# One-hot rows for the second pair of experts, sums in two groups of banks, and identity products in eleven waits of TensorE

## What is computed

```python
for i in range(2):                       # layers 0 and 1
    h = rmsnorm(x, norm_g[i])
    main = fox_attention(...) if i == 0 else retention(...)
    o = concat([main, mem_cross_attention(...)]) * silu(z)
    x = x + o @ w_out[i]
x = rmsnorm(x, final_norm_g)
h = rms_norm(x, mix_norm_g); y_a = short_conv_mixer(...); y_b = gated_deltanet(...)
x = x + concat([y_a, y_b]) @ w_out_2
h = rms_norm(x, ffn_norm_g)
# router: group of the largest logit, then the two best of its 8 experts, gates
# each expert, on blocks of its tokens:
y = (silu(xb @ w_gate[e]) * (xb @ w_up[e])) @ w_down[e]      # 1024 -> 512 -> 1024
x = x + sum over the token's experts of gate * y
return rms_norm(x, final_norm_g_2)
```

## Time and profile before

| | before |
|---|---|
| median of 3 runs, us | 1928.86 (1927.72 to 1931.02) |
| the profiled execution, us | 1930.05 |
| its span from the first to the last instruction, us | 1928.1 |
| PE / PE weight loads / DVE / ACT / POOL busy, us | 1799.9 / 1279.6 / 939.1 / 591.2 / 79.4 |
| mean clock granted to TensorE | 0.976 |
| HBM read and written, MB | 322.98 and 5.31 |

### The profile page before, as it was taken

One profiled execution on the slowest core, in us unless ns is written; L12 is line 12 of the kernel. 1 busy time (PEld: TensorE's weight loads), 2 busy tenths in 40 slices (PEclk: granted clock), 3 DMA queues, 4 the chain that ended last, 5 costly groups with the idle time before them and its releaser, 6 DMA issues.

```text
span 1928.1 us, 23485 instructions
## 1 busy us (share of the span) xinstructions
PE 1799.9 (93%) x9526; PEld 1279.6 (66%) x9526; DVE 939.1 (49%) x1559; ACT 591.2 (31%) x1054; POOL 79.4 (4%) x89
## 2 busy tenths in 40 slices
PE   6999999999988999999997999888977999999996
PEld 6878888888867777777766677788762333333332
DVE  4354555455465554445547565654661333333234
ACT  5433233332324322323335443423330111111112
POOL 0000000000000000000000000061011000000000
PEclk9999999999988999999998999989988999999999
DMA  6412222122212122222121122200379999999995
GB/s 253 167 66 88 88 77 99 66 99 99 99 66 77 66 88 77 79 96 77 66 88 66 55 100 87 88 1 12 130 283 357 421 420 420 420 421 420 420 421 239
DMA packets 50895, 325.91 MB, mean 169 GB/s; under 512 B 8163, under 2 KB 8339, under 8 KB 14176
## 3 DMA queue, kind: packets, MB, share of 16 engines
q1 hardware_dynamic: 44464, 305.65, 40.3%
q0 software_dynamic: 6176, 17.67, 2.6%
q10 hardware_dynamic: 144, 1.05, 0.1%
HBM read 322.98 MB, written 5.31 MB: 170 GB/s over the span
## 4 chain that ended last, share of the span: by engine, by line
PE 74%; DMA 9%; DVE 8%; ACT 4%; issue 3%; SPq 1%; POOL 1%; DVEq 0%; ACTq 0%; POOLq 0%
PE PJ L561 15%; PE PJ L563 15%; PE PJ L562 15%; PE PJ L2361 8%; PE PJ L2375 4%; DMA m_a<-in_w_moe 3%; DMA m_b<-in_w_moe 3%; PE PB L2387 3%; PE PB L2088 2%; DMA m_c<-in_w_moe 1%; PE PB L2166 1%; DVE x L1420 1%; PE PB L2049 1%; PE PB L2081 1%; PE PB L2180 1%
## 5 line engine op out<-in xcount | busy, mean ns | idle before, releaser
L561 PE MATMUL PJ<-hT_hi,w_hi 128*128 128x512 f32 x832 | 338.8, 407 | 7.5 <-DVE x L1420 6.1
L1218 DVE TENSOR_TENSOR w_lo<-w_raw,w_hi 128x1024 fp32r<-128x1024 f32 (+1 forms) x224 | 228.4, 1032 | 207.8 <-ACT w_hi L783 206.9
L563 PE MATMUL PJ<-hT_hi,w_lo 128*128 128x512 f32 x832 | 325.5, 391 | 0.0
L562 PE MATMUL PJ<-hT_lo,w_hi 128*128 128x512 f32 x832 | 325.0, 391 | 0.0
L783 ACT ACTIVATE w_hi<-w_raw 128x1024 fp32r<-128x1024 f32 (+1 forms) x224 | 196.2, 899 | 31.1 <-PE PJ L563 20.8
L561 PEld LDWEIGHTS PJ<-hT_hi,w_hi 128*128 128x128 f32 x832 | 156.8, 188 | 54.8 <-issue 20.7
L563 PEld LDWEIGHTS PJ<-hT_hi,w_lo 128*128 128x128 f32 x832 | 156.6, 188 | 34.2
L562 PEld LDWEIGHTS PJ<-hT_lo,w_hi 128*128 128x128 f32 x832 | 157.0, 189 | 33.4 <-issue 3.4
L837 ACT ACTIVATE sc<-sc,stats 128x256 f32<-128x256 f32 (+2 forms) x80 | 43.5, 544 | 325.9 <-DVE stats L1301 325.9
L1842 DVE TENSOR_TENSOR x<-x,PB 128x512 f32<-128x512 f32 x128 | 82.1, 684 | 111.3 <-PE PB L2387 111.2
L2361 PE MATMUL PJ<-m_b,xT 128*64 128x512 f32 x472 | 112.1, 604 | 2.7 <-DMA m_b<-in_w_moe 2.7
(11 more groups left out here) (408 smaller groups left out, 2778.2 us busy)
## 6 DMA issues: line engine op xcount, KB each, us to landing
w_raw<-in_w_all SPq DMA_DIRECT2D x92, 1024.0 KB, 4.8
m_b<-in_w_moe SPq DMA_DIRECT2D x88, 1024.0 KB, 26.4
m_a<-in_w_moe SPq DMA_DIRECT2D x71, 1024.0 KB, 26.3
m_c<-in_w_moe SPq DMA_DIRECT2D x22, 1024.0 KB, 26.7
m_d<-in_w_moe SPq DMA_DIRECT2D x11, 1024.0 KB
aux<-scr_c POOLq DMA_DIRECT2D x6, 512.0 KB, 4.3
aux<-in_decay POOLq DMA_DIRECT2D x6, 512.0 KB, 4.4
gbc<-in_gains POOLq DMA_DIRECT2D x4, 512.0 KB, 6.6
```

What stands on the lines that cost most here:

```text
L561: pe.matmul(dst, lh, rh, start=start, stop=False)
L562: pe.matmul(dst, lh, rl, start=False, stop=False)
L563: return pe.matmul(dst, ll, rh, start=False, stop=stop)
L1218: dve.tensor_tensor(w_lo[:, n % SPLIT, j * w:(j + 1) * w], w_raw[:, n % RAW, j * w:(j + 1) * w], w_hi[:, n % SPLIT, j * w:(j + 1) * w].bit ...
```

## The change

Eight edits. (1) Layer 0: slots 50 to 57 hang on the eight steps of the projections of g=7, 58 to 60 on panel `o` g=5, 61 to 66 on the first three steps of panel `o` g=6. (2) TensorE issues products of the identity with itself (`keep_clock`), whose result nobody reads, ahead of eleven waits. (3) Slot 16 (`m_d`) and `xs` change places in SBUF, so that panel 16 no longer waits for the first pair's rows; instead GpSimd's `memset` of `xs` waits for both pairs' rows (`x_tr` 2), and the table's read-back stands behind it. (4) `OH` has rows for four experts, the second pair's behind the first's; TensorE makes the second pair's rows out of them behind the panels of expert 1. (5) The gates of experts 0 and 1 come from sixteen one-column products of `OH` (`hg01`), so that `mid` of both needs no table; VectorE's part of the table (`table_out`) stands behind `mid` of expert 1. (6) `mid` is transposed into `PJ[1]`, and a pair's sums alternate between `PB[0:2]` and `PB[2:4]`, two row tiles at a time, behind the first and the third panel. (7) The last hidden transpose stands between the last but one expert's down panels. (8) At the end row tile 0 is multiplied by the gain on GpSimd and scaled on ScalarE, and written last. The blocks for experts with more tokens, under the condition, are a hardware loop on VectorE.

```diff
             if g == 1:
                 attach(range(u0 + 2, u0 + 10), new)
+            elif g == 7 and layer == 0:
+                attach(range(u0 + 50, u0 + 58), new)
...
         panel("o", 4, layer=layer, g=5)
         if layer == 0:
+            attach(range(u0 + 58, u0 + 61), steps[first:])
             panel("o", 4, layer=layer, g=6)
-            attach(range(u0 + 56, u0 + 64), steps[first:])
-            steps[-1]["slots"] += [u0 + 64, u0 + 65, u0 + 66]
+            attach(range(u0 + 61, u0 + 67), steps[first + 4:first + 7])
...
-                if n == 16:
-                    sp.wait_ge(x_tr, 1)
-                    for par in range(2):
-                        sp.wait_ge(hn_st[par], 16 * NT // 2)
...
-            for t in range(NT):
-                sp.wait_ge(s_x1, 5 + t)
+            for t in (1, 2, 3, 0):
+                if t:
+                    sp.wait_ge(s_x1, 4 + t)
+                else:
+                    sp.wait_ge(f_out, 1)
...
+            pool.wait_ge(x_tr, 2)
...
+            pool.memset(xs[:], 0.0).then_inc(r_set, 1)
+            pool.wait_ge(r_set, 4)
             pool.wait_ge(r_sc, 128)
...
-            for p in range(1, NPAIR):
-                if p >= 3:
+            for p in range(2, NPAIR):
+                if p >= 4:
...
+            pool.wait_ge(c_add, 8 * (NPAIR - 1) + 2)
+            pool.tensor_tensor(xs[:, 1, :], x[:, 0, :], gbc[:], ALU.mult).then_inc(f_xg, 1)
...
+            act.activation(x[:, 0, :], xs[:, 1, :], ACT.Copy, scale=rstd[:, 0:1]).then_inc(f_out, 1)
...
+            for i, o in enumerate((F["g01"], F["g1"])):
+                tt(o, F[f"E{i}"][:, :, 0:2], wide(gates[:, NT * i:NT * i + NT], 2), ALU.mult)
+            link(dve.tensor_tensor(F["g01"], F["g01"], F["g1"], ALU.add))
...
-            for t in range(NT):
-                for i in range(2):
+            for t, i in [(t, i) for pr in (0, 2) for t in range(NT) for i in (pr, pr + 1)]:
...
+                if e == 0:
+                    dve.wait_ge(m_mm, 1)
+                    dve.tensor_scalar(hg01, PB[0][:, 0:2], 0.5, None, ALU.mult).then_inc(r_hc, 1)
+                    dve.wait_ge(r_hc, 1)
                 hidden_mid(e % 2, e).then_inc(h_mid, 1)
+                if e == 1:
+                    table_out()
...
+            def keep_clock(bank, n):
+
+                for _ in range(n):
+                    pe.matmul(bank[:, 0:P], ident, ident, start=True, stop=True)
...
+                        if l == 0 and c < 3:
+                            keep_clock(PJ[0], (14, 5, 8)[c])
                         pe.wait_ge(g_bt, n + 1)
...
+                    if c == 0:
+                        keep_clock(PB[3], 24)
                     pe.wait_ge(g_vne, c + 1)
...
             def tile_transpose(n, t):
+                if (n, t) in ((3, 1), (5, 0), (5, 1)):
+                    if n == 3:
+                        pe.wait_ge(n_lo, 2 * (tiles_before[3] + 1))
+                    keep_clock(tile_bank(n, t, 0), {(3, 1): 9, (5, 0): 15, (5, 1): 10}[n, t])
...
             pe.wait_ge(s_id, 16)
+            keep_clock(PB[0], 20)
...
+                if s == last_o[0]:
+                    keep_clock(PB[0], 7)
                 products(s, middle)
...
+            keep_clock(PB[2], 22)
             pe.wait_ge(r_E, 1)
...
             def transpose_next(p):
-                pe.wait_ge(x_g[p % 2], 16 * ((p + 1) // 2))
+                if p == 1:
+                    pe.wait_ge(r_oh, 4 * NT)
+                    pe.wait_ge(r_hc, 1)
+                    pair_rows(1, (PB[0][:], PB[1][:]))
+                    return
+                pe.wait_ge(x_g[p % 2], 16 * (p // 2))
...
+            keep_clock(PB[2], 10)
             pe.wait_ge(r_oh, 2 * NT)
...
+            pair_rows(0, (PB[2][:], PB[3][:]))
+            for i in range(2):
                 for t in range(NT):
+                    for c in range(2):
+                        last = pe.matmul(PB[0][c * CAP:(c + 1) * CAP, i:i + 1], OH[:, t, i * CAP:(i + 1) * CAP],
+                                         F01[:, t, i:i + 1], start=(t == 0), stop=(t == NT - 1))
...
-                    if e % 2 and e >= 3:
+                    if e % 2 and e >= 3 and j % 2 == 0:
                         pair_combine((e - 3) // 2, j)
+                        pair_combine((e - 3) // 2, j + 1)
...
+                        if e == NE - 1 and j == 0:
+                            pe.wait_ge(h_mid, NE)
...
+                            hidden_transpose((NE - 1) % 2).then_inc(h_tr, 1)
```

174 lines of the change are left out of this document (108 added, 66 removed).

## The result

**Time.** Measured side by side, the changed kernel takes 1923.02 us (median of 6 runs, 1922.17 to 1924.81) and the kernel before 1930.65 (6 runs, 1927.72 to 1932.18). The ratio is 0.9965, with a 95% interval of 0.9955 to 0.9975: 7.6 us, where 9.2 were forecast, and inside the range of 1911 to 1926. The forecast of 1919.7 was taken off the 1928.86 of the first three runs; the kernel before came out 1.8 us higher in this measurement, so the two gains are to be compared, not the two times. The profiled execution has a span of 1920.9 us against 1928.1, so 7.2, at a mean granted clock of 0.989 against 0.976.

A forecast was written before the change was run, and what follows sets the result against it. Bound: TensorE's waits and half clock until the experts, then the expert panel queue at 420 GB/s. Terms -1.6 - 2.4 - 1.6 - 2.2 - 1.8 + 0.4 = -9.2 us off 1928.9 gave 1919.7, range 1911 to 1926.

The forecast's parts named there:

- Rival E: Whole kernel: the expert panel queue isn't what the end hangs on, the front part alone counts; chance 0.02.
- Rival D: In the filled waits: identity products run at half clock, 0.43 us each, making the kernel slower, 1948 us; chance 0.04.
- Inverse: In the inverse: identity products fit TensorE's mask waits, level 1 runs at full clock until masks are late; -1.6 us.
- Rival B: At the filled waits: the products fit but the clock falls nonetheless; only -3.6 us, so 1925.3; chance 0.10.
- Last heads of layer 0: End of layer 0: moved slots, panel `o` at full clock, less a clock falling in new waits; -2.2 us.
- First norm of layer 1: Nine products behind a new wait: second tile's transpose 3 us later, up to +0.9 against up to -1.8; 0 taken.
- Router: Ahead of the experts: products in two waits keep the first pair's rows at full clock; -1.3 us to the first expert.
- Steps (c) to (f): Experts: TensorE runs eight panels, second pair's rows, then waits for VectorE's copy behind the table (1474.2), until 1476.8.
- steps (b) and (g): Experts: gate products expose 0.4 us, panel 17 moves from 1447.6; second queue hole moved, panel 27 starts about 1482.5.
- step (a): Experts' start: panel 16 follows panel 15 at once, feeding the queue until 1443.5; 1.9 us from issue to bytes.
- Rival A: Expert stage: table read-back costs less or the hole closes; stage -5, attention -4, so 1914.7 us; chance 0.12.
- Rival C: Expert stage: read-back and gathers meet full panel queues, VectorE stands 3 us longer for the table; 1922.7 us; chance 0.14.

The follow-up runs named there:

- e5: Changed kernel with GpSimd's table read-back issued right behind the scatters, ahead of the zeroing of `xs`; 1918.74 us, ratio 0.9936 to the kernel before.
- e11: Changed kernel with early table read-back, no seven or nine identity products (nor the nine's new wait), 19 instead of 10 before the one-hot rows; 1914.22 us, ratio 0.9909.
- e1: Changed kernel without any of the 144 identity products, their waits kept; 1927.80 us, ratio 0.9981 to the kernel before.
- e7: Changed kernel with VectorE's blocks for experts with more tokens written out again instead of a hardware loop; 1926.85 us, ratio 0.9978 to the kernel before.
- e2: Changed kernel without the seven identity products ahead of the last panel `o` of layer 0; 1922.46 us, ratio 0.9959 to the kernel before.
- e6: Changed kernel with 19 instead of 10 identity products before the first one-hot rows; 1922.44 us, ratio 0.9957 to the kernel before.
- e10: Changed kernel with 26 more identity products in TensorE's idle time before expert 2; 1924.02 us, ratio 0.9964 to the kernel before.
- e8: Changed kernel with row tile 0 scaled by VectorE again and written first; 1925.26 us, ratio 0.9970 to the kernel before.

## Why the prediction was right, and where it was not

**Bound and method.** Right. Up to the router each saved microsecond of TensorE is found again at the next marks, and in the expert stage panels land one after another at 420 GB/s; the time is set by when the queue begins, its two holes and the end. Rival E fell with e5, where closing a hole of the queue brought 6.6 us.

**Price of an identity product.** Right where the clock is full: 20 records in 2.48 us, 18 in 2.28, so 0.25 us a product against the 0.22 forecast (0.23 in the long groups). Rival D fell. In the profiled execution one group alone ran slowly in part, the start's, whose first 19 records took 4.21 us.

**Recurrence: right**, -2.4, in each of the twelve executions that have the products. **First norm of layer 2: undersized**, -2.1 for -1.6, and equally steady: 35.95 to 35.97 us in twelve executions. There the term "until VectorE's splits are late" was taken too carefully.

**Inverse: oversized.** "Level 1 at full clock" came true in part and not always: 199.07 to 200.00 us over the executions, 200.08 before. On the average of the twelve with the products it is -0.65, and -1.6 was in none. Three waits of 1.0 to 1.2 us stand in a row behind the last fill, in executions where the clock held as in those where it fell. Where it held through level 1, as in e11, the gain was 1.0: the masks are late next, as forecast, and by more.

```profile
1255.56 0.66 PE L2224 MATMUL PB<-cst,bt 128*128 128x128 f32 x4 [1.16 <-POOL bt L715]
...
1260.59 3.61 PE L2226 MATMUL PB<-T,bt 128*128 128x128 f32 x24 [0.52 <-POOL bt L715]
```

Rival B holds for this group. (By its own condition, all but the attention and the expert stage's own part, its sum is -2.2 - 0.5 + 0.4 = -2.3, so 1926.6 and not 1925.3: the recorded figure keeps the router's 1.3, and the right one lies outside the stated range.) The page of the Trainium skill cited ahead ("TensorE: Matmul & The Clock Gate", What's actually happening) says that the monitor isn't in step with the kernel, and this case agrees, with numbers that the traces before could not give: the same instructions took 199.07 or 200.00 us in the inverse, 9.38 or 11.0 in the router, 108.8 or 110.4 at the last heads.

**Last heads of layer 0: oversized**, -0.9 for -2.2. That the seven products stand in the open was forecast; without them the slots are worth 0.8 to 1.8 us. The fall of the clock in the new waits (0.57 in the window from 556 to 560 us) was forecast as well. The step that failed is the place of the end, 572.1: the panel began at 573.5, in a trace that was 1.1 us ahead since the start, so 1.0 us later than before where 1.6 sooner was drawn, with 1.2 for the clock still to come. The two waits drawn as 4 and 2 us were 3.17 and 2.28; which part of the drawing is 1.4 us too short stays open.

**First norm of layer 1: wrong in size**, +1.5 for 0 with a bound of +0.9. The forecast put wait and products together at a push of 3 us. It is the products alone that cost, 1.0 to 1.7 us in this stretch, for the wait without them costs nothing (e1). The way is that named in the forecast: the second tile's transpose starts later, and ScalarE's squares for the fourth tile stand behind its copy (`xn` of the fourth tile begins 6.8 us after the norm's first split, for 5.1 before). The -1.8 on the other side did not come, though the last transposes ran wholly or partly at full clock in three executions (e7, e2, e6; 10.10 to 10.60 us): the clock was at half when layer 1's first products ran, in all fourteen.

**Start: not settled.** The -1.1 us stands where a 0 was forecast, but with the same code up to 469 us the first addition there comes at 466.4 to 469.7 us in twelve executions, and at 468.9 and 469.7 in the two without products. The scatter is larger than the difference.

**Router: wrong.** The -1.3 us of full clock for the first pair's rows did not come in the profiled execution (windows from 1430 to 1434 at 0.57). The step drew ten products, 2.2 us, into a wait of 2.95, and took it for granted that they hold. But the rank products ahead of them also ran at full clock (1.06 for 1.89 us) while VectorE needed as long as before, so the wait grew, and 2.26 us were left idle behind the ten. And where the clock did hold, in three other executions, next to nothing of it reached the end (e6): the step also took it for granted that a sooner first expert moves the stage.

**Experts: the mechanism right, the sum wrong.** Steps (c) to (f) came as drawn: six panels, no stop, second pair's rows, then 6.54 us idle (7 forecast), released by VectorE's copy behind the table, and a hole of the queue just before it. But the stage with the router is 0.9 us longer, not 1.8 shorter; 0.5 of this lies behind the first expert's first product. The failed steps are the router's 1.3 us and the two holes of the queue, which steps (b) and (g) made smaller than before and which, summed from the windows, are 0.6 and 0.8 us larger (more than the 0.5; the rest was not traced). For the first hole the reason is step (a): panel 16 ahead of the hole instead of inside it saves nothing, since the hole ends with panel 17. That the clock falls behind the idle time was left out; e10 shows that it explains at most 0.8 us of the hole and 0.2 of the time. Rival A fell: the read-back took 5.5 us for the 6.6 drawn, and the stage won nothing by it. Rival C was a case of this with a different cause; by its gain (6.2 us for the 7.6 measured) it is as near as the forecast's 9.2, but the table was not later than drawn: it came at 1468.6 in a trace that runs 5.8 us ahead, as 1474.2 had been forecast without these.

**Last hidden transpose:** +0.4 forecast, -0.05 measured. The wait for ScalarE's `mT` is indeed longer (0.97 for 0.60), and is given back ahead of it: from the last panel waited for to the end of the last transpose TensorE takes 15.9 us for 16.4, with the sums in two groups instead of four. That the grouping is the reason was not tested alone.

**The end: the unpriced edit.** The list of edits names a hardware loop for VectorE's further blocks, and no term of the sum has it. It brought 2.2 of the 7.2 us. The row that tells it was in the trace of before: VectorE idle for 2.38 us, put down to a root that had been there for 2.2. Row tile 0 itself was rightly put at nothing (e8).

So the sign and the range were right by their own steps for the recurrence and layer 2's norm, but the closeness of the sum, 9.2 for 7.6, is in good part luck: two errors of 2.7 and 2.3 us cancel, and so do most of the smaller ones.

## What to carry to other kernels

An engine's idle time that the profile puts down to an engine long done is worth a look of its own; here it was a jump over a long body of written-out blocks, 2.2 us that a loop took away. Filling a wait with idle products paid here in each execution where it left one short idle time (0.6 and 1.45 us), cost most of its length where the engine would have been let go (0.9 us of 1.7, and up to 1.7 of 2.3), and where it left 2.0 to 2.9 us, or three waits in a row, its gain changed from execution to execution. And a cheap instruction with a far-reaching wait, here a `memset` ahead of a read-back on the same queue, can cost more (6.6 us by the traces, 5.6 by the ratios) than all the fills bring together (3.1 by the ratios, with 0.4 to 5.8 possible): order a queue by who is waited for.

## What the runs showed of the hardware

The scatter between executions of one kernel is not spread evenly over it. Some stretches repeat to 0.04 us in twelve traces (35.95 to 35.97, 41.54 to 41.58), and 425 us of layer 1 to 0.2 in fourteen. The scatter sits in a few places: 9.38 or 11.0 us in the router, 108.8 or 110.4 at the last heads, 199.07 to 200.00 in the inverse, 1.5 us behind layer 1's norm, 3.3 us at the start of the kernel. A comparison of stretches between two traces therefore tells more than the medians of the totals, but only when it is known which values a stretch can take, and whether a gain in it reaches the end: the router's 1.6 us did not.

A branch that is not taken over fifteen written-out blocks on VectorE cost 2.23 and 2.38 us in two kernels; over a loop of one block none can be seen (the chain has 0.45 us for VectorE's sequencer at that place). The Trainium skill ("Advanced Engine Details and Errata", Control Flow Timing) gives about 108 ns for a compare-and-branch; by that figure the written-out blocks would have cost nothing worth a term, and the measurement decides against it for a jump this long, whose cause stays open.
